# Masking causal attention scores by a VectorE addition in PSUM instead of a TensorE matmul of the identity, with the softplus one unit later

## What is computed

```python
z = jnp.einsum('bhqd,bhkd->bhqk', qb, k)
strict = key_pos[None, :] < q_pos[:, None]
log_1m = jnp.where(strict, jax.nn.log_sigmoid(-z), 0.0)
rest = lax.cumsum(log_1m, axis=3, reverse=True) - log_1m
a = jnp.where(strict, jnp.exp(jax.nn.log_sigmoid(z) + rest), 0.0)
return jnp.einsum('bhqk,bhkd->bhqd', a, v)
...
x = x + swiglu(rms_norm(x, norm_ffn[i]), ffn_w_gate[i], ffn_w_up[i], ffn_w_down[i])
gate = jax.nn.sigmoid(rms_norm(x, ple_norm[i]) @ ple_w_gate[i])
x = x + gate * (p[i] @ ple_w_proj[i])
```

## Time and profile before

| | |
|---|---|
| median of 3 executions | 1246.95 us (1246.75 to 1247.27) |
| the profiled execution, own time | 1247.0 us |
| its span, first to last instruction | 1245.3 us |
| PE busy | 1236.6 us, 99% |
| DVE busy | 702.6 us, 56% |
| ACT busy | 623.2 us, 50% |
| POOL busy | 77.9 us, 6% |
| HBM | 184 GB/s over the span |

### The profile page before, as it was taken

One profiled execution on the slowest core, in us unless ns is written; L12 is line 12 of the kernel. 1 busy time (PEld: TensorE's weight loads), 2 busy tenths in 40 slices (PEclk: granted clock), 3 DMA queues, 4 the chain that ended last, 5 costly groups with the idle time before them and its releaser, 6 DMA issues.

```text
span 1245.3 us, 17289 instructions
## 1 busy us (share of the span) xinstructions
PE 1236.6 (99%) x5688; PEld 1028.3 (83%) x5688; DVE 702.6 (56%) x778; ACT 623.2 (50%) x752; POOL 77.9 (6%) x126
## 2 busy tenths in 40 slices
PE   9999999999999999999999999999999999999998
PEld 7888888888888888888888888888888788888886
DVE  6667566675765654555555555455545455545554
ACT  5458486684954544444444444444444444444443
POOL 0312103021000200000000000000000000002000
PEclk9999999999999999999999999999999999999999
DMA  7655555545455666666666666666565656565574
GB/s 262 203 166 160 164 174 163 184 152 163 152 179 184 185 194 193 186 187 185 198 188 188 187 185 194 189 187 186 181 203 174 193 181 208 165 210 161 195 216 137
DMA packets 120462, 229.24 MB, mean 184 GB/s; under 512 B 7490, under 2 KB 9844, under 8 KB 120436
## 3 DMA queue, kind: packets, MB, share of 16 engines
q1 hardware_dynamic: 119252, 226.80, 59.2%
q10 hardware_dynamic: 1184, 2.11, 0.5%
HBM read 226.78 MB, written 2.10 MB: 184 GB/s over the span
## 4 chain that ended last, share of the span: by engine, by line
PE 98%; issue 1%; DVE 0%; ACT 0%; DMA 0%; SPq 0%; ACTq 0%; DVEq 0%
PE acc L903 93%; PE T L917 2%; PE T L931 1%; PE Z L931 1%; PE R L954 1%; DMA x<-in_x 0%; ACT w_hi L389 0%; PE acc L1015 0%; PE Z L944 0%; DVE w_lo L621 0%; PE R L955 0%; DVE stage L867 0%; DVE x L870 0%; DVE neg_log_1m L674 0%; ACT softplus L448 0%
## 5 line engine op out<-in xcount | busy, mean ns | idle before, releaser
L621 DVE TENSOR_TENSOR w_lo<-raw,w_hi 128x1024 fp32r<-128x1024 f32 (+1 forms) x448 | 528.9, 1189 | 413.6 <-ACT w_hi L389 411.6
L389 ACT ACTIVATE w_hi<-raw 128x1024 fp32r<-128x1024 f32 (+1 forms) x448 | 455.5, 1020 | 547.2 <-PE acc L903 521.2
L903 PE MATMUL acc<-w_hi,xT_hi 128*128 128x512 f32 x1216 | 477.8, 393 | 0.0
L903 PE MATMUL acc<-w_hi,xT_lo 128*128 128x512 f32 x1216 | 473.9, 390 | 0.0
L903 PE MATMUL acc<-w_lo,xT_hi 128*128 128x512 f32 x1216 | 473.2, 389 | 0.0
L903 PEld LDWEIGHTS acc<-w_hi,xT_lo 128*128 128x128 f32 x1216 | 228.2, 188 | 48.1
L903 PEld LDWEIGHTS acc<-w_lo,xT_hi 128*128 128x128 f32 x1216 | 228.5, 188 | 46.1
L903 PEld LDWEIGHTS acc<-w_hi,xT_hi 128*128 128x128 f32 x1216 | 228.4, 188 | 45.9 <-ACT stage L586 0.2
L903 PE MATMUL acc<-w_hi,hT_hi 128*128 128x512 f32 x352 | 137.5, 391 | 0.5 <-DVE w_lo L621 0.5
L903 PE MATMUL acc<-w_hi,hT_lo 128*128 128x512 f32 x352 | 137.0, 389 | 0.0
L903 PE MATMUL acc<-w_lo,hT_hi 128*128 128x512 f32 x352 | 137.0, 389 | 0.0
(11 more groups left out here) (121 smaller groups left out, 654.7 us busy)
## 6 DMA issues: line engine op xcount, KB each, us to landing
raw<-in_sb_w_in SPq DMA_DIRECT2D x96, 512.0 KB, 3.7
raw<-in_ffn_w_gate SPq DMA_DIRECT2D x88, 512.0 KB, 3.7
raw<-in_ffn_w_up SPq DMA_DIRECT2D x88, 512.0 KB, 3.7
raw<-in_ffn_w_down SPq DMA_DIRECT2D x80, 512.0 KB, 4.8
raw<-in_sb_w_out SPq DMA_DIRECT2D x32, 512.0 KB, 4.1
raw<-in_ple_w_gate SPq DMA_DIRECT2D x20, 512.0 KB, 5.1
raw<-in_ple_w_gate SPq DMA_DIRECT2D x24, 256.0 KB, 3.3
raw<-in_ffn_w_down SPq DMA_DIRECT2D x16, 256.0 KB, 3.1
```

The source lines that it names most:

```text
L389: act.activation(w_parts[0][:, slot(u), 0:n, :], raw[:, slot(u), 0:n, :], ACT.Copy).then_inc(hi_ready, 1)
L621: dve.tensor_tensor(w_parts[1][:, slot(u), 0:n, :], raw[:, slot(u), 0:n, :], w_parts[0][:, slot(u), 0:n, :].bitcast(F32), ALU.subtract).th ...
L903: last = pe.matmul(acc[pair][tb][:, :], parts[a][:, c, tb * P:(tb + 1) * P], w_parts[w][:, slot(u), i, :], start=(start and i == 0 and n = ...
```

## The change

The mask leaves TensorE. `unseen` becomes an ordinary fp32 tile, 128 x 2 x 128, that GpSimd fills at the start; the fp32r copies `unseen` and `ident_r` and the three VectorE copies that made them are gone. `scores` begins with the products themselves. A new VectorE step `mask_scores` adds `unseen` to the two diagonal blocks of `Z` in place and signals `z_masked`, for which `softplus_of` waits now. It stands behind `lo` at u = every*h + 3, where `log_terms` stood; `softplus_of` and `log_terms` move to u = every*h + 4 (`L_AT`). `R_AT` and `W_AT` stay.

```diff
--- before.py
+++ after.py
@@ -97,7 +97,7 @@
 
 
     A_EVERY, B_EVERY = 3, 2
-    R_AT, W_AT = 3, 6
+    L_AT, R_AT, W_AT = 4, 3, 6
 
     with ExitStack() as ctx:
         def sb(name, shape, dt=F32, where=ctx):
@@ -149,8 +149,6 @@
             weight_parts = [[at_row(f"weight{i}_hi", [P, 3 * P], F32R), at_row(f"weight{i}_lo", [P, 3 * P], F32R)] for i in range(2)]
             later = at_row("later", [P, P], F32R)
             ones = at_row("ones", [P, P], F32R)
-            unseen = at_row("unseen", [P, 2, P], F32R)
-            ident_r = at_row("ident_r", [P, P], F32R)
             p_sb = at_row("p_sb", [P, TB, KP * P])
             mix_rows = at_row("mix_rows", [KD, P])
             gain_rows = at_row("gain_rows", [2 * KD + 2, P])
@@ -158,7 +156,8 @@
             softplus = at("softplus", [P, 3 * P])
             neg_log_1m = at("neg_log_1m", [P, 3 * P])
             weight = [at(f"weight{i}", [P, 3 * P]) for i in range(HG)]
-            masks = at("masks", [P, 3, P])
+            masks = at("masks", [P, 2, P])
+            unseen = at("unseen", [P, 2, P])
         hT = [row("hT_hi", [P, KF, SEQ], F32R), row("hT_lo", [P, KF, SEQ], F32R)]
 
         acc = [[ctx.enter_context(nc.psum_tensor(f"acc{i}{tb}", [P, NT], F32)) for tb in range(TB)] for i in range(2)]
@@ -194,6 +193,7 @@
         head_ssq_ready = sem("head_ssq_ready")
         head_scale_ready = sem("head_scale_ready")
         z_ready = sem("z_ready")
+        z_masked = sem("z_masked")
         act_step = sem("act_step")
         softplus_ready = sem("softplus_ready")
         z_free = sem("z_free")
@@ -293,15 +293,15 @@
             pool.affine_select(out=ident[:, :], in_=ident[:, :], compare_op=ALU.not_equal, fill=1.0,
                                base=0, pattern=[[-1, P]], channel_multiplier=1).then_inc(consts_ready, 1)
             pool.memset(masks[:, 0:2, :], 1.0).then_inc(zeroed, 1)
-            pool.memset(masks[:, 2, :], 0.0).then_inc(zeroed, 1)
+            pool.memset(unseen[:, :, :], 0.0).then_inc(zeroed, 1)
             pool.memset(minus_half[:, :], -0.5).then_inc(zeroed, 1)
             pool.wait_ge(zeroed, 4)
 
             pool.affine_select(out=masks[:, 0, :], in_=masks[:, 0, :], compare_op=ALU.is_gt, fill=0.0,
                                base=0, pattern=[[-1, P]], channel_multiplier=1).then_inc(consts_ready, 1)
 
-            pool.affine_select(out=masks[:, 2, :], in_=masks[:, 2, :], compare_op=ALU.is_gt, fill=MASKED,
-                               base=0, pattern=[[1, P]], channel_multiplier=-1).then_inc(consts_ready, 1)
+            pool.affine_select(out=unseen[:, :, :], in_=unseen[:, :, :], compare_op=ALU.is_gt, fill=MASKED,
+                               base=0, pattern=[[0, 2], [1, P]], channel_multiplier=-1).then_inc(consts_ready, 1)
 
             def inverse_root(r, ms, n, step):
 
@@ -439,7 +439,7 @@
 
             def softplus_of(h):
 
-                act.wait_ge(z_ready, h + 1)
+                act.wait_ge(z_masked, h + 1)
                 act.wait_ge(z_free, h)
                 act.activation(softplus[:, :], Z[:, 0:3 * P], ACT.Abs).then_inc(act_step, 1)
                 act.wait_ge(act_step, 2 * h + 1)
@@ -466,7 +466,7 @@
                         keep_o(g * HG + h)
                     if u == every * h + R_AT + 4:
                         weights_of(g * HG + h, h)
-                    if u == every * h + 3:
+                    if u == every * h + L_AT:
                         softplus_of(g * HG + h)
 
             def group(g, first=False):
@@ -666,6 +666,12 @@
                                              in1=v[0][:, tb, :].bitcast(F32), op0=ALU.mult,
                                              op1=ALU.subtract).then_inc(acc_free[0][tb], 1)
 
+            def mask_scores(h):
+
+                own = Z[:, 0:3 * P].rearrange("p (b q) -> p b q", q=P)[:, 0:3:2, :]
+                dve.wait_ge(z_ready, h + 1)
+                dve.tensor_tensor(own, own, unseen[:, :, :], ALU.add).then_inc(z_masked, 1)
+
             def log_terms(h, i):
 
                 neg = neg_parts[i % 2]
@@ -707,8 +713,10 @@
                         weights_lo(g * HG + h, h)
                     if u == every * h + R_AT + 3:
                         exponent(g * HG + h, h)
-                    if u == every * h + 3:
+                    if u == every * h + L_AT:
                         log_terms(g * HG + h, h)
+                    if u == every * h + L_AT - 1:
+                        mask_scores(g * HG + h)
 
             def group(g, first=False):
                 U0 = A0 + g * AU
@@ -728,9 +736,7 @@
                                           ALU.subtract).then_inc(T_free[0], 1)
                     if first and u == DU + 1:
                         dve.wait_ge(consts_ready, 3)
-                        for part, value in ((later[:, :], masks[:, 0, :]), (ones[:, :], masks[:, 1, :]),
-                                            (unseen[:, 0, :], masks[:, 2, :]), (unseen[:, 1, :], masks[:, 2, :]),
-                                            (ident_r[:, :], ident[:, :])):
+                        for part, value in ((later[:, :], masks[:, 0, :]), (ones[:, :], masks[:, 1, :])):
                             dve.tensor_copy(part, value).then_inc(parts_ready, 1)
                     if first and 1 <= u <= DU:
 
@@ -939,10 +945,7 @@
                 q = [part[:, i, :] for part in qT]
                 k = [part[:, i, :] for part in kT]
 
-
-                own = Z[:, 0:3 * P].rearrange("p (b q) -> p b q", q=P)[:, 0:3:2, :]
-                pe.matmul(own, ident_r[:, :], unseen[:, :, :], start=True, stop=False, skip_group_check=True)
-                three(Z[:, 0:2 * P], [a[:, 0:P] for a in k], q, False, False)
+                three(Z[:, 0:2 * P], [a[:, 0:P] for a in k], q, True, False)
                 three(Z[:, 2 * P:3 * P], [a[:, P:2 * P] for a in k], [a[:, P:2 * P] for a in q],
                       False, True).then_inc(z_ready, 1)
 
@@ -1021,7 +1024,7 @@
             turn_input(1)
             keep_busy(WARM[1])
             group(0, first=True)
-            pe.wait_ge(parts_ready, 5)
+            pe.wait_ge(parts_ready, 2)
             with nc.Fori(1, GROUPS, engines=[mybir.EngineType.PE], hint_back_edge=True) as g:
                 group(g)
 
```

## The result

The changed kernel takes **1289.27 us** (median of 6, 1285.21 to 1294.71) against 1247.11 (median of 6): ratio 1.0336, 95% interval 1.0313 to 1.0359. The forecast was 1278, 1270 to 1285. Slower was right, but the loss is 42.2 us where 31 was forecast: a third more, and 4.3 us above the range. The profiled execution took 1290.41 us.

The account below looks back on a forecast made before the run. TensorE, busy 1236.6 of 1245.3 us, was taken as the bound. Waits of 26.9 us in stage A and 6.9 in stage B, less 2.2 for the identity matmuls, gave +31.6 on 1247.0: forecast 1278, range 1270 to 1285.

Parts of the forecast that it names:

- The bound: Whole kernel: TensorE bounds it, busy 1236.6 of 1245.3 us, so every wait put into its list lengthens the run.
- The chain of 8.56 us: ScalarE and VectorE, from a unit's end through softplus and log terms until `neg_lo` reaches TensorE: 8.56 us.
- a wait of 2.49 in heads 1 to 3 of stage A: TensorE ahead of `rest`: 8.56 us less 6.07 of its own work, 7.5 us in a group.
- the hand-over: From the end of the releasing step to TensorE's next start: 0.15 us.
- Head 0: Stage A, first head of a group: `neg_lo` reaches TensorE at 91.48, `rest` due at 90.66, a 0.8 us wait.
- The transposes behind head 3: Stage A, u = 12: `norm_heads` stands behind head 3's log terms, so TensorE's transposes of `normed` wait 0.65 us more.
- Stage B: `scores` waits for `Z` to be freed: 2.2, 3.35 and 1.3 us more behind heads 0, 1 and 2, together 6.9.
- The identity: TensorE: 16 identity matmuls removed, each saving between 0.11 and 0.17 us, 2.2 us taken in all.
- The clock falls: Rival: 12 waits of TensorE each halve the clock for one unit, 2.72 us each, 33 us, 1311 us; 6%.
- The addition on VectorE: 16 additions of 128x256 in PSUM, 0.4 to 0.8 us each: no cost at 0.42, 1.2 us at 0.8.
- Loads twice as long: Rival: each ScalarE table load holds the chain another 1.28 us, 26 loads, 33 us more, 1311 us; 1%.
- Loads that run ahead: Rival: ScalarE loads tables ahead of `hi` while waiting for TensorE, chain shrinks to 6.0 us, 1246.5 us; 3%.

Follow-up runs that it names:

- e7: The changed kernel with unused 512-column matmuls filling TensorE's waits in both stage A and stage B; 1278.29 us, ratio 1.0251.
- e2: The kernel before, mask still an identity matmul, with softplus and log terms moved behind unit every*h + 4; 1293.02 us, ratio 1.0364.
- e1: The changed kernel, mask on VectorE, with softplus and log terms back behind unit every*h + 3; 1249.55 us, ratio 1.0019.

## Why the prediction missed

**What held.** The bound, the mechanism and the side. The chain of 8.56 us behind the end of a unit, against 6.07 for TensorE, was to give a wait of 2.49 in heads 1 to 3 of stage A; it measured 2.38 (the start of `rest`, 2.49 us behind the last matmul ahead of it, less 0.11 without a wait). The 0.11 too much is the hand-over: 0.15 us was taken from a `scores`, and `rest` starts 0.05 behind `neg_lo`. Head 0: 0.8 forecast, 0.62 and 0.1 of slower starts behind the wait measured. The transposes behind head 3: 0.65 forecast, 0.62. Stage B: 2.2, 3.35 and 1.3 forecast; ahead of `scores` the distance of starts grew from 0.70, 0.22 and 0.27 us to 2.80, 3.48 and 1.44, so by 2.1, 3.3 and 1.2. All of these are high by 0.03 to 0.2. The identity is off to the other side: 2.2 forecast, 16 times 0.12, so 1.9 measured. It is partly luck that the sum fits the kernel whose clock is held up: from the first `scores` to the same matmul of stage B behind the attention e7 takes 311.0 us (81.92 to 392.90) against 281.2 before (81.76 to 362.94), 29.8 more, and the medians differ by 31.1, where 31 was forecast.

**The step that failed** is the clock, which the sum puts at nothing. The prediction had it as the rival *The clock falls*, with 6%, on the grounds that "the waits are short beside the 8 us of dense work between them". The clock fell behind waits of 2.2 us with 10 us or more of dense work between them, six times in the profiled execution; that is the sign of being wrong that the prediction named, matmuls further apart than 0.23 us behind a wait. It should have been part of the forecast, since the earlier trace rows had no wait over 2 us and so no evidence against it. The Trainium skill's rule that I set beside it (TensorE: Matmul & The Clock Gate, Part 1) is now supported: idleness halved the rate (starts 0.43 us apart instead of 0.23) and work restored it. My price for that rival was wrong the other way, 12 falls of 2.72 us, 33 in all: it fell behind six of the twelve, and cost 11.0 us by the medians (e7 against the changed kernel), 11.9 by the two profiles (the same stretch, 322.9 us against 311.0).

**A cost put at nothing.** The addition on VectorE: right in the changed kernel (e2), where the softplus waits for a unit's end anyway. The cover is the delay itself. Without the delay the addition stands in the softplus's path and costs more than the identity matmuls it saves: 3.4 us against 1.9 in e1's profile. The choice in this change lies between 2 us of loss by one way (e1) and 42 by the other.

**The other rivals.** Loads twice as long: refuted, each load is 1.28 us and the next activation follows at once, in the changed kernel too. Loads that run ahead: refuted, `hi` waits 4.18 us at 108.82 and the load still comes behind it at 109.90.

**What stays open.** Which wait brings the clock down. Waits of equal length did and didn't, in one profile and between kernels; the runs of the changed kernel spread from 1285 to 1295 us with mean clocks of 0.993 to 0.984. I have shown that idleness is the cause, not the rule by which it acts.

## What to carry to other kernels

When a step on a helper engine moves one unit later, don't ask how busy that engine is; ask behind which wait it now stands, add up everything between that wait and the signal TensorE needs (table loads and the neighbours' steps included), and compare with what TensorE has to do meanwhile. If the sum makes a dense TensorE wait again and again, as here for 2.2 to 3.1 us, count a clock loss on top (here a third of the net loss of the chains), and widen the range upward for its chance. Look for a short second wait close behind the first; unused matmuls in a wait that can't be removed held the clock here. A cheap operation that leaves TensorE for a dependent chain is not free just because the receiving engine is half idle: 0.12 us a head saved on one engine, 0.42 us and a hand-over added to the other's path.

## What the hardware showed that I had not expected

- Waits of 2.2 us brought the granted clock to its lower level for stretches of up to nearly 7 us, with matmuls 0.43 us apart instead of 0.23, in a kernel that keeps TensorE 97% busy.
- The same wait (3.1 us in stage B) left the clock at 1.00 in one kernel and brought it to 0.77 over 15 us in another that differs only ahead of it.
- Filling the waits with 87 unused matmuls in stage A and 30 in stage B took 11 us off the kernel.
- In place, the addition of 128x256 in PSUM takes 0.42 us, the same as the nearest operation that writes SBUF.
